# Eleven pairs of products with h by Strassen's rule, in a stage of their own

## What is computed

```
h     = rmsnorm(x, norm_pre) * (1 + scale) + shift          # scale, shift, gate from silu(c) @ w_ada
u_pool, z_pool, u_ssm, z_ssm, g_pool, g_ssm = h @ w_in      # six blocks of 1024 columns
y_pool = pool_w (mean of the last 2/4/8/16 tokens - token) * pool_scale * silu(z_pool)
s      = complex diagonal state space over u_ssm, 64 groups of 16 channels with 64 states
y_ssm  = gelu(Re(C s) + D u) ; y_ssm *= sigmoid(y_ssm @ glu_w + glu_b) ; y_ssm *= silu(z_ssm)
merged = sigmoid(g_pool) * (y_pool @ w_branch_pool) + sigmoid(g_ssm) * (y_ssm @ w_branch_ssm)
out    = x + gate * rmsnorm(merged @ w_out, norm_post)
```

## Time and profile before

| | |
|---|---|
| median of 3 runs | 1047.91 us (1045.55 to 1048.6) |
| the profiled execution, its own time | 1046.91 us |
| its span, first to last instruction | 1045.1 us |
| PE busy | 988.6 us, 4644 matmuls |
| DVE busy | 537.1 us |
| ACT busy | 322.1 us |
| POOL busy | 38.4 us |
| DMA, mean over the span | 123 GB/s, 128.27 MB |
| mean granted clock of TensorE | 0.985 |

### The profile page before, as it was taken

One profiled execution on the slowest core, in us unless ns is written; L12 is line 12 of the kernel. 1 busy time (PEld: TensorE's weight loads), 2 busy tenths in 40 slices (PEclk: granted clock), 3 DMA queues, 4 the chain that ended last, 5 costly groups with the idle time before them and its releaser, 6 DMA issues.

```text
span 1045.1 us, 11347 instructions
## 1 busy us (share of the span) xinstructions
PE 988.6 (95%) x4644; PEld 828.8 (79%) x4644; DVE 537.1 (51%) x724; ACT 322.1 (31%) x329; POOL 38.4 (4%) x82
## 2 busy tenths in 40 slices
PE   1988999899999989998999999999999999999997
PEld 1876788788888878887878888888888888887885
DVE  6958365685767678578542221251213324446233
ACT  5622033543453354344531101141113222214111
POOL 0059000000000000000000000000000000000000
PEclk9999899999999989998999999999999999999999
DMA  9621445437336533723762222231111116331322
GB/s 348 254 94 61 170 140 135 118 110 189 97 88 153 171 81 110 184 70 95 244 244 76 101 103 99 101 121 41 45 56 41 59 63 262 122 139 41 121 81 80
DMA packets 70197, 128.27 MB, mean 123 GB/s; under 512 B 18945, under 2 KB 41089, under 8 KB 70145
## 3 DMA queue, kind: packets, MB, share of 16 engines
q1 hardware_dynamic: 70144, 127.55, 38.2%
HBM read 91.87 MB, written 27.26 MB: 114 GB/s over the span
## 4 chain that ended last, share of the span: by engine, by line
PE 66%; DVE 14%; DMA 6%; SPq 6%; ACT 5%; issue 3%; DVEq 0%; ACTq 0%
PE ps L1332 54%; PE ps L1472 8%; SPq L576 2%; DVE w_lo L988 1%; PE psa L1400 1%; ACT w_hi L766 1%; DMA coef_d<-coef 1%; PE ps L1422 1%; SPq L652 1%; DMA raw<-in_wstream 1%; DMA k_d<-ks 1%; SPq L635 1%; DMA u_in<-u_d 1%; ACT pool_hi L856 1%; DMA in_raw<-yp_d 1%
## 5 line engine op out<-in xcount | busy, mean ns | idle before, releaser
L1332 PE MATMUL ps<-h_hi,w_hi 128*128 128x512 f32 x896 | 280.8, 395 | 11.2 <-DVE w_lo L988 9.5
L1332 PE MATMUL ps<-h_lo,w_hi 128*128 128x512 f32 x896 | 277.9, 391 | 0.0
L1332 PE MATMUL ps<-h_hi,w_lo 128*128 128x512 f32 x896 | 277.8, 391 | 0.0
L1332 PEld LDWEIGHTS ps<-h_hi,w_hi 128*128 128x128 f32 x896 | 168.3, 190 | 46.1 <-DVE w_lo L988 10.6
L1332 PEld LDWEIGHTS ps<-h_lo,w_hi 128*128 128x128 f32 x896 | 169.5, 189 | 35.8
L1332 PEld LDWEIGHTS ps<-h_hi,w_lo 128*128 128x128 f32 x896 | 169.3, 189 | 35.7
L988 DVE TENSOR_TENSOR w_lo<-raw,w_hi 128x1024 fp32r<-128x1024 f32 x72 | 87.8, 1222 | 174.7 <-ACT w_hi L766 174.7
L766 ACT ACTIVATE w_hi<-raw 128x1024 fp32r<-128x1024 f32 x72 | 75.8, 1054 | 131.2 <-PE ps L1332 70.1
L801 ACT ACTIVATE gt<-ps 128x1024 f32<-128x1024 f32 x31 | 31.8, 1026 | 160.3 <-PE ps L1332 160.2
L1332 PE MATMUL ps<-in_hi,w_hi 128*128 128x512 f32 x256 | 79.3, 391 | 1.2 <-DVE w_lo L988 1.2
L1332 PE MATMUL ps<-in_lo,w_hi 128*128 128x512 f32 x256 | 78.8, 389 | 0.0
(11 more groups left out here) (237 smaller groups left out, 1014.6 us busy)
## 6 DMA issues: line engine op xcount, KB each, us to landing
raw<-in_wstream SPq DMA_DIRECT2D x80, 512.0 KB, 3.8
ada<-in_w_ada SPq DMA_DIRECT2D x8, 1024.0 KB, 18.2
x_tok<-in_x SPq DMA_DIRECT2D x8, 512.0 KB, 7.2
u_d<-u_out SPq DMA_DIRECT2D x8, 512.0 KB, 3.1
u_in<-u_d SPq DMA_DIRECT2D x64, 64.0 KB, 2.7
cos_t<-st SPq DMA_DIRECT2D x16, 256.0 KB, 4.3
sin_t<-sw SPq DMA_DIRECT2D x16, 256.0 KB, 4.9
y_d<-y_act SPq DMA_DIRECT2D x64, 64.0 KB, 2.1
```

The lines of the kernel that those rows point to most:

```text
L1332: last = mm(ps[slot(u)][:, f * HALF:f * HALF + HALF], a[s][:, k, :], b[:, k, f * HALF:f * HALF + HALF], start=k == 0 and q == 0, stop=k == ...
```

## The change

22 of the 48 products with h are put in eleven pairs: (us 0, 1) to (us 6, 7), (gp 0, 1) to (gp 6, 7), and (zs 1, 2), (zs 3, 4), (zs 5, 6). A pair is a product of a weight matrix of 1024 by 256 with h; its 2x2 blocks are multiplied by Strassen's rule in Winograd's form, in seven block products P1 to P7 of 12 matmuls each (4 slices of input channels, 3 passes, 128 output channels, 512 tokens). h is held in four quarters (`bop`); quarter 1 (B12) is stored to DRAM and reloaded after the stage, and four sums of quarters (T1 to T4: t_hi, t_lo) are made once. Four sums of weight blocks (pair_sum) and seven adds of PSUM results (`added`) are VectorE's for each pair, and one copy (`copied`) and seven high parts are ScalarE's. The block products go through a ring of five PSUM banks and a ring of eight operand slots. The eleven pairs run one after the other. VectorE makes the input and output weights, the first cosine and sine tables and the taps in places between (CHUNKS, `prepare`), TensorE runs part_a1 and part_a2 there, and SyncE stores all of it to DRAM.

After it, the second stage runs up and zp for each block, with the state-space products, the pool products, and loads of what was stored; then come zs7, the eight bp (whose gates gp and zs come back from DRAM), and gl, bs and out as before. The toep tile and its copy on ScalarE are gone: taps are loaded in their final order. `split_lo` of the third product has buffers of its own (wx_hi, wx_lo), and in the first stage the coefficient steps on VectorE are cut up between the `split_lo`. The coefficients' small steps are the same. Cut to its core:

```diff
-N_GS = 7
-USES = [("gs", n) for n in range(N_GS)] + [("us", 0)]
...
+FIRST = [("gs", n) for n in range(KT)] + [("zs", 0)]
+PAIRS = [("us", a) for a in range(0, KT, 2)] + [("gp", a) for a in range(0, KT, 2)] + [("zs", a) for a in (1, 3, 5)]
+NP = len(PAIRS)
+USES, JOBS = list(FIRST), list(FIRST)
+for m in range(KT):
+    USES += [("up", m), ("zp", m)]
+    JOBS += [("up", m)] + ([("pp", m - 2), ("pp", m - 1)] if m in (2, 4, 6) else []) + [("zp", m)]
...
+P1, P2, P6, P5, P3, P4, P7 = range(7)
+S_ORDER = [(j, i) for j in range(NP) for i in (P1, P2, P6, P5, P7, P4, P3)]
+S_POS = {u: n for n, u in enumerate(S_ORDER)}
+RING, BANKS = 8, 5
+
+ADDS = {P6: 1, P2: 2, P7: 3, P4: 5, P5: 6, P3: 7}
+CHUNKS = [("cos", 0), ("sin", 0)]
+for b in range(KT):
+    CHUNKS += [("in", b), ("out", b)]
+TABLE_AT = {0: [("cos", 1), ("sin", 1)], 1: [("cos", 2)], 2: [("sin", 2)], 3: [("cos", 3)], 4: [("sin", 3)]}
+CHUNK_AT, n = {}, 0
+for j in range(NP - 1):
+    for place in ("a",) if j in (0, 9) else ("a", "b"):
+        CHUNK_AT[j, place] = CHUNKS[n]
+        n += 1
```

TensorE: a block product, the order in a pair, and the second stage:

```diff
+            def half_product(j, i):
+                o = 7 * j + i
+                pe.wait_ge(pair_lo, o + 1)
+                n = S_POS[j, i]
+                if n >= BANKS:
+                    free(*S_ORDER[n - BANKS])
...
+                bank = banks[n % BANKS]
...
+                for k in range(4):
...
+                    for q, (a, b) in enumerate(((a_hi, b_hi), (a_hi, b_lo), (a_lo, b_hi))):
+                        last = mm(bank, a, b, start=k == 0 and q == 0, stop=k == 3 and q == 2)
+                last.then_inc(st_done, 1)
...
+            for j in range(NP):
+                half_product(j, P1)
+                part_a(CHUNK_AT.get((j - 1, "b")))
+                half_product(j, P2)
+                half_product(j, P6)
+                half_product(j, P5)
+                part_a(CHUNK_AT.get((j, "a")))
+                half_product(j, P7)
+                half_product(j, P4)
+                half_product(j, P3)
...
+            for m in range(KT):
+                even = m % 2 == 0
+                product(("up", m), h)
+                if even and m:
+                    pool_pair_ready(m // 2 - 1)
+                    pool_product(m - 2)
+                part_b(m)
+                if even and m:
+                    pool_product(m - 1)
+                if m:
+                    part_c(m - 1)
...
+                product(("zp", m), h)
```

ScalarE, one pair:

```diff
+                copy_p1(j)
+                if j:
+                    pair_high(j, P4)
+                    pair_high(j, P7)
+                if more:
+                    pair_high(j + 1, P1)
+                    pair_high(j + 1, P2)
+                prep_out(CHUNK_AT.get((j - 1, "b")))
+                if more:
+                    pair_high(j + 1, P6)
+                    pair_high(j + 1, P5)
+                    pair_high(j + 1, P3)
...
+                if kind != "us":
...
+                    act.wait_ge(added, 7 * j + 6)
+                    fn(rt[j % 2][:, :], rt[j % 2][:, :], func, scale=scale).then_inc(func_done, 1)
+                    act.wait_ge(added, 7 * j + 7)
+                    fn(gt[j % 2][:, :], gt[j % 2][:, :], func, scale=scale).then_inc(func_done, 1)
```

VectorE, one pair:

```diff
+                if j:
+                    c12(j - 1)
+                    sum3(j)
+                    pair_low(j, P4)
+                    pair_low(j, P7)
+                if more:
+                    pair_low(j + 1, P1)
+                prepare(CHUNK_AT.get((j, "a")))
+                u2(j)
+                c11(j)
+                if more:
+                    pair_low(j + 1, P2)
+                    sum1(j + 1)
+                    sum2(j + 1)
+                    sum4(j + 1)
+                    pair_low(j + 1, P6)
+                    pair_low(j + 1, P5)
+                u3(j)
+                c12_first(j)
+                if more:
+                    pair_low(j + 1, P3)
+                else:
...
+                    split_lo(USE["up", 0])
+                    split_lo(USE["zp", 0])
+                prepare(CHUNK_AT.get((j, "b")))
+                c21(j)
+                c22(j)
+            c12(NP - 1)
```

VectorE, second stage:

```diff
+            for m in range(KT):
+                i, p, even = m // 2, USE["up", m], m % 2 == 0
+                if even and m:
+                    yp_out(m - 2)
+                pooling(m)
+                if even and m:
+                    yp_out(m - 1)
                 split_lo(p + 2)
...
+                rotate_in(m)
+                pool_low(m)
+                if even:
+                    pool_weights_low(i)
+                for chunk in TABLE_AT.get(m, ()):
+                    prepare(chunk)
                 split_lo(p + 3)
...
+                rotate_out(m)
```

ScalarE, head of a block in the second stage:

```diff
+                evac(("up", m), by_residue(pu), ACT.Copy)
                 split_hi(p + 2)
...
+                swap_x(m)
```

SyncE, from the last pair to the second stage:

```diff
+            load_wout(0)
+            pair_read(NP - 1)
...
+            load_win(0)
             load_u(0)
...
+            store_pair(NP - 1)
+            sp.wait_ge(taps_zero, 1)
+            load_taps(0)
+            sp.wait_ge(st_done, len(S_ORDER))
+            load_tables(0)
+            load_cfp(1)
+            load_pw(0)
+            load_u(1)
+            load_tables(1)
+            load_w(USE["up", 1])
+            load_w(USE["zp", 1])
```

SyncE, storing one block's taps:

```diff
+                    sp.wait_ge(k_ready, b + 1)
+                    for j in range(CH):
+                        sp.dma_start(k_d[b][:, :, j, :], ks[SG * j:SG * j + SG, :, :]).then_inc(k_stored, 16)
+                    if b + 1 < KT:
+                        load_cf(b + 1)
```

More of the change, by code:

```diff
@@ L919, in _ @@
+            split_hi(USE[following[0]])
+            split_hi(USE[following[1]])
             act.wait_ge(y_loaded, 16 * KT)
             for n in range(KT):
[L921 to L926 removed]
+                fn(y_hi[:, n, :], y_raw[:, n, :], ACT.Copy).then_inc(in_hi_done, 1)
@@ L928, in _ @@
+            for u in following[2:]:
+                split_hi(USE[u])
             for n in range(KT):
                 act.wait_ge(yz_done, KT)
+                act.wait_ge(job_out[slot(("bp", 7))], evicted(("bp", 7)))
                 if n >= 2:
@@ L1064, in bcast @@
+            t_sums(2)
+            dve.wait_ge(tabled, 1)
+            t_sums(3)
+            split_lo(8)
+            for k in range(1, 4):
+                t_low(k)
             def bcast(ap, axis, n):
@@ new lines, in c11, with u3, c12_first, c21 @@
+            def c11(j):
+                c = c_tiles(j)
+                add(j, P2, c[0], c[0], 1)
+            def u3(j):
+                c = c_tiles(j)
+                add(j, P7, c[3], c[1], 1)
+            def c12_first(j):
+                c = c_tiles(j)
+                add(j, P5, c[1], c[1], 3)
+            def c21(j):
+                c = c_tiles(j)
+                add(j, P4, c[2], c[3], 3)
+            def c22(j):
+                c = c_tiles(j)
+                add(j, P5, c[3], c[3], 5)
@@ new lines, in c12 @@
+            def c12(j):
+                c = c_tiles(j)
+                add(j, P3, c[1], c[1], 4)
+            sum1(0)
+            sum2(0)
+            pair_low(0, P1)
+            pair_low(0, P2)
+            sum4(0)
+            for i in (P6, P5, P3, P4):
+                pair_low(0, i)
+            sum3(0)
+            pair_low(0, P7)
+            for j in range(NP):
+                more = j + 1 < NP
+                if j:
+                    c12(j - 1)
[18 more added lines that the diff above has]
+                    pair_low(j + 1, P3)
+                else:
+                    dve.wait_ge(b12_hi, 1)
+                    tt(bop[:, 1, 1, :, :], b12[:, :, :], bop[:, 1, 0, :, :].bitcast(F32), ALU.subtract).then_inc(b12_lo, 1)
+                    split_lo(USE["up", 0])
[3 more added lines that the diff above has]
+                c22(j)
@@ L1218, in m1_out, with in_low @@
+            yp_out(6)
+            def in_low(n):
+                dve.wait_ge(in_hi_done, n + 1)
+                src = yp_in[n] if n < FROM_TILE else rt[n % 2][:, :]
+                tt(hb(1, n), halves(src), hb(0, n).bitcast(F32), ALU.subtract).then_inc(in_lo_done, 1)
+            for n in range(3):
+                in_low(n)
+            yp_out(7)
+            for n in range(3, KT):
+                in_low(n)
             def m1_out(n):
-                dve.wait_ge(job_out[slot(("gp", n))], evicted(("gp", n)))
+                dve.wait_ge(gp_in, 16 * n + 16)
```

1133 lines of the change are left out of this document (675 added, 458 removed).

## The result

The changed kernel takes 1067.5 us (median of 4 runs, 1064.6 to 1071.0), the kernel before 1047.8 beside it: ratio 1.0193, 95% interval 1.0151 to 1.0235. It is slower, by 1.9%: the whole interval lies above 1, but whether it is more or less than 2% stays open. I had forecast 1002 us.

What follows compares the result with a forecast made beforehand. TensorE was taken to bound the kernel: span 1045.1 - 29.9 - 38.0 = 977.2, plus losses 1.1, 5.0, 15.5 and 1.5 = 1000.3, plus 1.8 beyond the span, said as 1002 us; range 984 to 1025.

Steps and rivals of the forecast that it cites:

- The matmuls, 29.9: Strassen stage: 84 matmuls a pair instead of 96, eleven pairs save 132; at 0.2269 us each, 29.9 us less.
- All losses of before come back, 38.0: TensorE's 38.0 us lost before bs in the old kernel are regained; losses of the new stages are added separately.
- From block 2 on VectorE keeps up ... rotate_out ends 4 or more before part_c: Second stage: VectorE's 26.2 us in block 4 fit TensorE's 32.7; in block 3, 21.9 against 27.2.
- SyncE adds to it ... in_weights waits 0.8 to 1.8: Strassen stage, gp and zs pairs: stores, cf and bc take SyncE 8.4 us against 6.6 to 7.6 of VectorE.
- The loop: Strassen stage, gp and zs pairs: c22 through ScalarE and VectorE to c22, 21.8 to 24.2, middle 23.0, against TensorE's 21.5.
- From the last pair to block 1, 15.5: Start of second stage: 2.7 us before up0, then rotate_out late for part_c of block 0, 3.0 low clock; 15.5 lost.
- bp stage, 1.5: bp stage: in bp4 to bp7 yz waits for zs loads, gl0's split_lo comes late; 1.5 us lost, ends 0 and 6.
- First stage, 1.1: First stage: gs2 waits only for ScalarE to evacuate gs0 from PSUM slot 0, about 1.1 us lost.
- that VectorE bounds the Strassen stage: Rival, chance 0.15: small VectorE instructions take 0.75 us with waits, the loop 25.2, the kernel 1023 us.
- that the clock falls by cycling through five banks: Rival, chance 0.05: bank waits drop TensorE's clock in the Strassen stage; time 1002 + 229 s, at a third 1078 us.

Runs made afterwards that it cites:

- e6: Changed kernel with the edits of e1 to e4, plus yz put behind split_lo and gate_sum and the five PSUM banks dealt anew: 995.4 us, ratio 0.951.
- e7: e6 with the first block product of each of the eleven pairs computed twice, bringing back 132 matmuls: 1022.8 us, ratio 0.9776.
- e1: Changed kernel with the pooling-weight load issued one block earlier on SyncE's queue: 1040.7 us, ratio 0.9936.
- e11: e6 without the edit of e1, so the pooling weights load at the old place of the queue: 1023.9 us, ratio 0.9772.
- e3: Changed kernel with the next cf and bc loads issued before the eight stores of the taps in the Strassen stage: 1052.2 us, ratio 1.0042.
- e2: Changed kernel with up1's and zp1's loads moved up the queue and pair 1's tables made behind rotate_out(0): 1053.4 us, ratio 1.0044.
- e4: Changed kernel with bp2's weights loaded ahead of the eight loads of y: 1063.2 us, ratio 1.0142.

## Why the prediction was wrong

- **The matmuls, 29.9**: right. Where nothing waits, the 84 of a pair take 19.04 us (e6, 142.73 to 161.77; by 0.2269 each 19.06), and e7 priced the 132 at 27.4.
- **All losses of before come back, 38.0**: the waits for u_in and for the low weights of the first stage did. New ones of the same kind took their place.
- **"From block 2 on VectorE keeps up ... rotate_out ends 4 or more before part_c"**: this step failed. I summed VectorE's instructions (26.2 against 32.7) and never asked when each may begin. In blocks 2, 4 and 6 rotate_out ended 7.1 to 7.8 us after TensorE had come to part_c, since pool_high and swap_z stood behind pw_hi on ScalarE. The diff showed load_pw behind y_done, taps, u and yp, and pw_hi ahead of pool_high and swap_z. In the kernel before, the load had a lead of 64 to 67 us over its use in these blocks, and ScalarE never waited there. Its queue and ScalarE, kernel before:

```profile
315.72 0.43 SPq L685 DMA_DIRECT2D pw_raw<-in_pool  x1
```

```profile
379.90 0.62 ACT L885 ACTIVATE pw_hi<-pw_raw 128x512 fp32r<-128x512 f32 x1
```

  The change gave that lead up: 4.4 us from issue (492.69) to use (497.07), late three times. The prediction put this at nothing; it was worth 26.7 us (e1), 28.6 (e11).
- **"SyncE adds to it ... in_weights waits 0.8 to 1.8"**: the right loop, mis-sized. Eight stores of 8 KB took 6.41 us to issue; I had priced them by the eight taps loads, 3.86. The wait was 2.92. The loop came out at the forecast 23.0 in two pairs; what I had mis-sized is the clock behind the waits for v, which made two other pairs 29.65 and 26.94. The stage lost 21.1 with the join, not 7.7. Worth 15.3 (e3).
- **"From the last pair to block 1, 15.5"**: right in its places and nearly in its size. Before up0 2.90 (2.7 said), then 3.34 at up1 and 8.72 at part_c(0), 12.1 where I had 9.8; e2 gave 14.1 without touching the first, so 17.0 in all.
- **"bp stage, 1.5"**: the zs loads were seen, the eight y loads ahead of bp2 not. 15.5 lost. e4's edit alone gave 4.2, near the noise; in e6 7.1 is still lost, of it 6.1 in four waits for low weights, and no run tried to mend those.
- **First stage, 1.1**: 4.4, since gs2 waits 2.28 for ScalarE to empty gs0's bank, with a granted clock of 0.56 in the 2.25 us behind it.
- **The rivals**: that VectorE bounds the Strassen stage fell with e3 and e7, that the clock falls by cycling through five banks with e6, whose 77 block products ran at 1.00. The 0.05 that I gave to slower was this last rival alone; I had one load late in its queue, up1's, and none of my cases had the pooling weights'.

## What to carry to other kernels

An engine at 62% busy says nothing of when its work may begin: for each instruction that waits for a DMA, find that DMA's place in the queue, and what stands in line behind the waiting instruction. When a change moves a load, write down its lead over its use before and after. A load with a free buffer belongs ahead of the stores and of the waits that it doesn't need.

## What the runs showed of the hardware

- Eight stores of 8 KB took 6.4 us to issue, 0.80 each; of the loads of 512 KB shown above, wout took 0.32, the weights 0.55 and zs 0.57. Issued right behind cf and bc (e3) they took 5.1, and bc 1.7 instead of 0.66: the sum for the nine is 6.8 against 7.1, so what was moved was the order, not the work.
- A wait of 7 to 8 us cost TensorE 2.6 us beyond itself (e11 against e6). A shorter one can cost more: with a wait of 2.85 us, and part_a's small matmuls behind it, a pair took 29.65 us instead of 21.8, the granted clock at 0.50 from 279 to 285 us. In e6 the longest wait from the first pair on is 2.4, before gl0, with a granted clock of 0.67 in the 4 us behind it; no slice of its clock is under 0.9.
